# One table of turns for the ten mixer strands of a three-mixer transformer kernel

## The reference

```python
x = x + 0.5 * swiglu(rms_norm(x, ffn1_norm[l]), ffn1_w_gate_up[l], ffn1_w_down[l])
u = rms_norm(x, mix_norm[l]) @ w_in[l]
u_ssd, u_ml, u_rw = split(u)
y = concatenate([ssd_mixer(u_ssd, ...), mlstm_mixer(u_ml, ...), rwkv7_mixer(u_rw, ...)])
x = x + y @ w_out[l]
x = x + 0.5 * swiglu(rms_norm(x, ffn2_norm[l]), ffn2_w_gate_up[l], ffn2_w_down[l])
```

## Time and profile before

| what | before |
|---|---|
| median of 3 runs | 1774.94 us (1774.27 to 1777.12) |
| span of the profiled execution | 1774.2 us; no separate time is given for it |
| granted TensorE clock, mean | 0.98 |
| PE busy | 1709.9 us in 13812 instructions |
| DVE, ACT, POOL busy | 1288.9, 931.2, 411.8 us |
| mixer stage, layer 0 and layer 1 | about 205 to 498 us and 916 to 1208 us |

### The profile page before, as it was taken

How to read it: one execution, slowest core, us unless ns; L and a number is a source line. 1 busy time by engine, 2 the same in 40 slices (tenths; PEclk the granted TensorE clock), 3 DMA queues, 4 the chain that set the end, 5 groups by cost and what they waited for, 6 DMA issues and landing times.

```text
span 1774.2 us, 32697 instructions
## 1 busy us (share of the span) xinstructions
PE 1709.9 (96%) x13812; PEld 1535.5 (87%) x13812; DVE 1288.9 (73%) x2141; ACT 931.2 (52%) x1666; POOL 411.8 (23%) x316
## 2 busy tenths in 40 slices
PE   8999999999899999999999999989999999989998
PEld 6888988887798888888898888779888898979987
DVE  5887775855567887688777576566787776789974
ACT  5774436323446764577443532344676455556652
POOL 2772000000213761167200000021376200021110
PEclk9999999999899999999999999989999999989999
DMA  6675622211146665666562220115665543335442
GB/s 254 240 276 193 219 95 96 76 45 49 49 167 247 232 239 175 218 248 227 188 216 95 96 96 29 47 49 170 215 250 207 195 175 120 119 143 190 172 152 105
DMA packets 45057, 282.67 MB, mean 159 GB/s; under 512 B 6128, under 2 KB 6768, under 8 KB 18544
## 3 DMA queue, kind: packets, MB, share of 16 engines
q1 hardware_dynamic: 44912, 280.60, 44.1%
HBM read 279.53 MB, written 1.05 MB: 158 GB/s over the span
## 4 chain that ended last, share of the span: by engine, by line
PE 84%; DVE 10%; ACT 3%; POOL 1%; issue 1%; DMA 1%; SPq 0%; DVEq 0%; ACTq 0%
PE banks L527 27%; PE banks L528 14%; PE banks L1062 8%; PE banks L519 7%; PE banks L521 7%; PE banks L520 7%; PE banks L1669 4%; DVE WL L490 2%; ACT WH L485 1%; PE banks L1938 1%; DVE XC L1131 1%; PE banks L566 1%; DMA ring<-wst 1%; PE banks L1948 0%; PE banks L734 0%
## 5 line engine op out<-in xcount | busy, mean ns | idle before, releaser
L490 DVE TENSOR_TENSOR WL<-ring,WH 128x2048 fp32r<-128x2048 f32 (+1 forms) x219 | 459.8, 2111 | 111.1 <-ACT WH L485 111.0
L527 PE MATMUL banks<-XNP,WH 128*128 128x512 f32 x1408 | 498.3, 399 | 10.7 <-DVE XNP L612 8.5
L485 ACT ACTIVATE WH<-ring 128x2048 fp32r<-128x2048 f32 (+1 forms) x223 | 380.7, 1715 | 54.1 <-PE banks L521 46.6
L528 PE MATMUL banks<-XNP,WL 128*128 128x256 f32 x1408 | 393.0, 279 | 0.0
L527 PEld LDWEIGHTS banks<-XNP,WH 128*128 128x128 f32 x1408 | 266.1, 189 | 72.4 <-DVE XNP L612 9.0
L960 POOL TENSOR_TENSOR HP<-G,HP 128x256 fp32r<-128x256 f32 x110 | 210.1, 1911 | 309.3 <-ACT HP L772 309.3
L527 PE MATMUL banks<-HP,WH 128*128 128x512 f32 x770 | 267.5, 392 | 0.8 <-POOL HP L960 0.7
L528 PEld LDWEIGHTS banks<-XNP,WL 128*128 128x128 f32 x1408 | 266.8, 189 | 0.0
L528 PE MATMUL banks<-HP,WL 128*128 128x256 f32 x770 | 215.2, 280 | 0.0
L1062 PE MATMUL banks<-XN,ring 128*128 128x256 f32 x832 | 200.8, 389 | 0.0
L1062 PEld LDWEIGHTS banks<-XN,ring 128*128 128x128 f32 x832 | 155.4, 194 | 21.6 <-issue 0.7
(11 more groups left out here) (496 smaller groups left out, 3281.4 us busy)
## 6 DMA issues: line engine op xcount, KB each, us to landing
ring<-wst SPq DMA_DIRECT2D x205, 1024.0 KB, 4.8
ring<-wst SPq DMA_DIRECT2D x80, 704.0 KB, 4.2
LP<-lp SPq DMA_DIRECT2D x1, 1872.0 KB, 7.2
LP<-lp SPq DMA_DIRECT2D x4, 448.0 KB, 5.5
ring<-wst SPq DMA_DIRECT2D x2, 512.0 KB, 5.5
X<-xin SPq DMA_DIRECT2D x2, 512.0 KB, 6.2
out<-X SPq DMA_DIRECT2D x4, 256.0 KB, 2.2
C<-cst SPq DMA_DIRECT2D x1, 193.0 KB, 4.9
```

The costliest lines, as they stand in the source:

```text
L485: e.do.activation(WH[:, slot[q], 0:n], ring[:, i % NSLOT, 0:n], ACT.Copy).then_inc(*w_act.up("high", q))
L490: e.do.tensor_tensor(WL[:, slot[q], 0:n], ring[:, i % NSLOT, 0:n], WH[:, slot[q], 0:n].bitcast(F32), ALU.subtract).then_inc(*w_dve.up("low ...
L527: e.do.matmul(b[:, :], WH[:, s, cols], x.rearrange("p s t -> p (s t)"), start=first, stop=False)
L528: return e.do.matmul(b[:, 0:T], WL[:, s, cols], x[:, 0, :], start=False, stop=last)
```

## The change

`order_of` and its rules go. The list is written out as a text, `MIXER_TURNS`, with `name*n` for n turns in a row; `turns` unfolds it, and an assertion sees that every strand gets as many turns as it has. No generator, semaphore, buffer or instruction differs. The two lists have the same first 15 turns and differ from the 16th on.

```diff
-def order_of(steps):
-    turns = ["proj", "rwkv", "rwkv more", "lane0", "proj more", "lane1", "ahead first", "scan more", "ssd", "proj end", "lane2", "scan", "lane3", "ssd",
...
-    return in_turns(steps, turns, needs, allowed)
+MIXER_TURNS = """
+proj*22 scan proj scan proj*8 scan*2 rwkv proj rwkv proj scan proj scan*3 proj scan proj rwkv proj*2 rwkv scan
...
+fin ssd fin*2 ahead*4 fin ahead*2
+"""
+
+
+def turns(text):
+
+    out = []
+    for word in text.split():
+        name, n = (word.split("*") + ["1"])[:2]
+        out.extend([name] * int(n))
+    return out
...
-            orders[l] = order_of(steps) if l < DEPTH else second_order_of(steps)
+            orders[l] = turns(MIXER_TURNS) if l < DEPTH else second_order_of(steps)
+            assert all(orders[l].count(name) == n for name, n in steps.items())
```

More of the change, by code:

```diff
@@ L206, in in_turns @@
     return out
-def order_of(steps):
-    lanes = [f"lane{j}" for j in range(4)]
-    turns = ["proj", "rwkv", "rwkv more", "lane0", "proj more", "lane1", "ahead first", "scan more", "ssd", "proj end", "lane2", "scan", "lane3", "ssd",
[L212 to L265, removed]
-    return in_turns(steps, turns, needs, allowed)
@@ L290, in second_order_of @@
     return in_turns(steps, turns, needs)
+MIXER_TURNS = """
+proj*22 scan proj scan proj*8 scan*2 rwkv proj rwkv proj scan proj scan*3 proj scan proj rwkv proj*2 rwkv scan
+proj*2 rwkv proj scan rwkv proj scan proj*2 scan*2 rwkv*2 proj*2 rwkv proj scan*2 rwkv proj scan proj rwkv scan
+proj*4 scan proj*2 rwkv scan rwkv*2 proj scan proj lane3 lane2 scan lane0 lane1 ssd proj scan proj ssd proj
+lane3 lane0 lane1 lane2 lane0 lane2 scan lane0 lane1 rwkv lane3 scan proj ssd scan proj scan ssd proj ssd lane0
+lane2 lane1 ssd scan ssd proj lane2 lane3 lane1 lane2 lane0 ssd proj scan*2 ssd proj lane1 lane3 lane2 lane3
+lane0 lane1 lane2 ssd scan proj scan*2 proj ssd scan lane3 lane1 lane2 ssd scan ssd proj lane3 lane0 lane1
+lane0 ssd scan proj ssd proj ssd proj ssd scan proj lane1 lane0 ssd scan lane0 lane2 lane1 scan ssd proj lane1
+lane3 scan lane0 ssd lane0 lane1 lane3 ssd proj scan lane3 lane2 lane1 scan*2 proj lane3 lane2 lane0 lane1
+lane3 scan lane2 lane0 lane1 lane3 lane0 lane2 ssd lane0 lane3 lane2 ssd proj*2 lane2 lane3 lane1 ssd ahead
+scan proj scan proj lane2 proj*3 lane3 lane0 scan lane1 lane2 proj lane0 lane1 lane2 ssd lane0 lane3 ssd*2 scan
+lane2 lane0 lane1 proj lane3 lane2 lane0 lane1 lane3 lane0 lane3 ssd lane0 lane3 ssd scan ssd lane2 lane1 ssd
+lane3 ssd lane1 lane2 lane3 lane1 lane2 lane3 lane0 lane1 ssd lane2 proj scan lane0 lane1 ssd ahead lane2 lane3
+fin ssd fin*2 ahead*4 fin ahead*2
[6 more added lines that the diff above has]
+    return out
 def hybrid_kernel(nc, xin, wst, lp, sp2, cst, out):
```

## The result

The changed kernel runs in 1724.3 us (median of 4 runs, 1723.7 to 1725.9) against 1776.0 us of the kernel before beside it; the ratio is 0.9712, with a 95% interval of 0.9700 to 0.9724: 51.7 us or 2.9% faster. Predicted were 1735 us, 2.2%, with a range of 1720 to 1766. A second comparison with more runs gave 1724.15 us and 0.9709 (0.9696 to 0.9722).

The account below looks back on a forecast made before the run. PE bounds the kernel, busy 1709.9 of 1774.2 us. The terms 17.7 + 6.3 + 6.2 + 3.7 + 2.6 - 2.8 - 3.0 + 9 = 39.7 give 1734.5, as a median 1735 us, range 1720 to 1766.

Parts of the forecast that it names:

- the likeliest case: The forecast itself, with no rival holding: 1735 us, spanning 1725 to 1745, chance 0.60.
- Tile changes: PE in both mixers: 104 fewer meetings of 64x64 matmuls with others, 0.17 us each, gain 17.7 us.
- The alternative that the prediction weighed: The 0.34 us belongs to the projection's own first rows, as many as before; the sum would be 17.7 us smaller.
- The wait behind the last head: PE's wait for the SSD sum (L2059), queued on DVE behind the last mLSTM head, goes: 3.2 + 3.1 = 6.3 us.
- The wait behind the gating: PE's wait for a lane's copy on ACT (L1763), behind SSD's gating: 8.2 us less 1.0 per layer, 6.2.
- The wait for POOL: PE's wait for summed squares (L2093), late behind POOL's 3.39 us subtraction: 2.3 + 1.8, leaving 0.2 per layer, gain 3.7 us.
- The early part: Early mixers: waits at L1519 and L1669 go, +2.6 us; scan vector steps ahead of DVE's decay settings cost -2.8.
- the charge: PE waits 1.4 us per layer at the gate matmuls (L1502), as scan steps precede DVE's decay settings: -2.8 us.
- New small waits at the end: Final copies of three lanes queue on ACT behind normalised SSD tiles: 1.5 us per layer, -3.0.
- The clock: End of the mixers: PE's granted clock, fallen after the 3.2 and 4.1 us waits, recovers 9 of 13.6 us.
- the end only reshuffles: Rival: the three long waits of the last 50 us return elsewhere with the fallen clock; 1757 us, chance 0.18.
- waits in the packs: Rival: where lane steps follow each other, DVE is late and the 17.7 us goes into waits; 1753 us, chance 0.14.

Follow-up runs that it names:

- the first run: Changed kernel with projection halves moved into the packs of lane steps, 56 more tile-size changes in all: 1737.2 us, ratio 0.9778.
- the second run: Changed kernel with projection halves and lane turns moved, 114 more tile-size changes in all, as many as the kernel before: 1743.1 us, ratio 0.9820.
- the new end behind the old body: Order of the kernel before up to the last mLSTM head (scan turn 42), then what is left in the changed kernel's order: 1773.6 us, ratio 0.9984.

## Why the prediction was right, and where its terms were off

The direction, the range and the mechanism in the main held, and the time came out 10.7 us below the forecast, outside the 1725 to 1745 given for the likeliest case by less than a microsecond. Term by term:

- **Tile changes, 17.7 us.** Measured 18.7 with all of them put back, at 0.164 us apiece (0.17 predicted, from two pairs of rows); 17.1 is what the change leaves for them once the clock is taken out (below). Between the two I had let myself be led to 0.12 by the spacings of groups in the traces, in the expectation of the first run; the second run decides for 0.16. The alternative that the prediction weighed, a cost bound to the projection's first rows, is out.
- **The wait behind the last head, 6.3 us.** Gone in full, and worth 6.6 us as a wait when put back. But the prediction's reason, that the head only has to stand further ahead, holds only within the whole table: moved alone it passes its 3.8 us on to the next in DVE's queue, as a wait of 3.1. It also counted too few lane steps behind the head, eight; the table has eleven, and PE's work there runs from 417.45 to 427.58 us in layer 0, 10.1 us and not some 9.
- **The wait behind the gating, 6.2 of 8.2.** All 8.2 gone. The leftovers of 1.0 us in each layer did not appear.
- **The wait for POOL, 3.7.** 4.2 gone. The cause was not quite as I had it (below).
- **The early part, +2.6 and -2.8.** This step failed: the waits of 0.7 and 0.6 went, 2.5 us, and the charge was not paid; there is no wait at L1467 (before L1502), though the vector step of the earlier trace rows does stand elsewhere now, at 252.8 us. Taken alone, the early part is worth nothing, since other waits come in its place. I had found what is queued behind the step, but not whether anyone needs it soon.
- **New small waits at the end, -3.0.** The size was right (2.4), the place wrong: PE waits for DVE's new state (L1780), not for ACT's copies.
- **Left out:** the four waits for L1760, 2.7 us, and two of 0.2 us at L1948 also went.
- **The clock, 9 of 13.6.** Over the whole run (1 - clock) x busy, taken over each stretch at 0.50, is 24.8 us before and 12.0 after, in the mixers 15.0 and 1.7. So 12.8 us of PE's 29.9 are clock, and 17.1 are left for the tile changes, within 1.1 us of the 18.2 of the run that put them back. The prediction's 13.6 is the 15.0 read from windows of ten microseconds (its terms for layer 0 add up to 6.7, not 6.8). Its reason failed: "only after PE stood idle for microseconds" is wrong in the kernel before already. In each layer one of three falls, 1.7 us, stands behind no wait but behind 16 rows of one column, with PE busy all the time (last section); the prediction counted it with the fall behind the wait of 3.2 us. That these two falls went as well, with the same 16 rows still there at 434.0 and 1115.8 us, is luck as far as the prediction goes.

The waits come to 21.9 us against a net 13.0, and PE's busy time to 29.9 against 26.7: 51.8 us against 39.7. Of the 12.1 us between them, 5.8 are charges that were not paid (8.2 set for what the new order might break, 2.4 measured), 3.1 are waits that I had left out, and 3.2 are PE's busy time. Most of the charges named a queue and a reason, but no row. Of the rivals, "the end only reshuffles" is what happens with a single turn moved, and with the new end behind the old body; neither it nor waits in the packs happened in the table as a whole, because its end was written for the progress that its own body leaves.

## What to carry to other kernels

In an in-order queue shared by many strands, a wait is not a property of the turn that shows it: moving that turn hands the wait to its neighbour, and half of a good order can be worth nothing with the other half missing. Judge an order as a whole, by how much other work stands between each step and its reader. Where PE is full, count how often its tile size changes, since each change costs some 0.16 us that no wait shows; and look at what a wait does to the clock behind it, which here, net, was two thirds of the wait again.

## What the runs showed of the hardware

- The clock fell behind narrow rows too, with no idle time ahead of it. In the changed kernel it does so in layer 1, in both of its profiled executions: PE is busy from 950 to 965 us, and shortly behind 16 rows of two columns (1.84 us) the clock reads 0.92 and then 0.73 (0.82 and 0.84 in the other execution), though wide rows stand on both sides:

```profile
955.71 1.84 PE L1475 MATMUL banks<-C,RV 128*128 128x2 f32 x16
```

```profile
955.00:960.00 5.00, 5.00 (x37) 4.55 (x36) 4.62 (x16) 4.44 (x10) 0.00 (x0) 0.92 0.31 131
960.00:965.00 5.00, 5.00 (x19) 4.15 (x18) 0.92 (x3) 1.12 (x3) 0.00 (x0) 0.73 0.10 18
```

  The kernel before does it behind 16 rows of one column, again with PE busy throughout:

```profile
448.52 1.95 PE L1266 MATMUL banks<-C,XC 128*128 128x1 f32 x16
```

```profile
450.00:452.00 2.00, 2.00 (x31) 1.77 (x32) 0.42 (x2) 0.01 (x1) 0.00 (x0) 0.83 0.00 0
452.00:454.00 2.00, 2.00 (x16) 1.61 (x13) 1.76 (x10) 0.86 (x4) 0.00 (x0) 0.50 0.00 0
```

  Such a fall costs 1.7 us. It does not come every time: the same 16 rows of the changed kernel stand in layer 0 at 275.6 us, and the clock stays at 1.00. What decides it, no run here shows. The Trainium skill, TensorE: Matmul & The Clock Gate, "Why this matters for your kernels", names idle gaps; these rows show that the clock can fall behind busy time too.
- DVE stops for POOL, and POOL, it seems, for DVE. In the changed kernel both waits of L1677 in layer 0 stand behind DVE settings of 64 columns that last over a microsecond while POOL runs, and end as POOL's instruction ends (timelines of DVE and POOL):

```profile
440.89 0.57 DVE L1771 TENSOR_SCALAR RV<-YV,KP 128x64 f32<-128x64 f32 x3
...
443.84 1.34 DVE L1771 TENSOR_SCALAR RW<-YV,KP 128x64 f32<-128x64 f32 x1
...
446.09 1.12 DVE L1771 TENSOR_SCALAR RV<-YV,KP 128x64 f32<-128x64 f32 x1
...
449.32 0.25 DVE L1771 TENSOR_SCALAR RW<-YV,KP 128x64 f32<-128x64 f32 x1
```

```profile
443.83 1.31 POOL L2056 TENSOR_TENSOR XE<-XE 128x512 f32<-128x512 f32 x1 [243.11 <-ACT XE L1968]
...
445.89 1.27 POOL L2056 TENSOR_TENSOR XE<-XE 128x512 f32<-128x512 f32 x1
```

The setting that starts at 443.84 ends at 445.18, POOL's at 445.14; that of 446.09 ends at 447.21, POOL's at 447.16. Alone the same instruction takes 0.25 us. It seems to work the other way too: POOL's subtraction of 3.39 us takes 0.73 us in the changed kernel (at 447.92), and it stood beside DVE's gating of 2.36 us, two inputs in SBUF, and two subtractions of DVE right behind that (L1452, until 468.28). So the wait for POOL that I put down to POOL's own slowness was, as far as rows show it, DVE's lock; no run here moved the one away from the other. The Trainium skill, SBUF — State Buffer, "Who interferes with whom", says that the two share a pair of ports and that the second to start is stopped for the whole instruction; the rows of DVE beside POOL agree.
